# Level products of a chunked recurrence on four quadrants of TensorE, and rows of v turned once, stored and loaded by chunk

## The reference, cut to what matters

```python
def wkv_scan(s0, r, w, k, v, a, b, reverse):
    def step(s, inp):
        r_t, w_t, k_t, v_t, a_t, b_t = inp
        sa = jnp.einsum('bhvk,bhk->bhv', s, a_t)
        s = s * w_t[:, :, None, :] + sa[..., :, None] * b_t[:, :, None, :] \
            + v_t[..., :, None] * k_t[:, :, None, :]
        return s, jnp.einsum('bhvk,bhk->bhv', s, r_t)
```

## Time and profile before

| What | Value |
|---|---|
| median of 3 runs | 2602.45 us (2600.98 to 2603.02) |
| the profiled execution's own time | 2604.29 us |
| its span in the profile | 2602.5 us |
| its mean granted TensorE clock | 0.933 of full speed |
| PE busy over the span | 2314.5 us (89%) |
| DVE busy | 1688.6 us (65%) |
| ACT busy | 1025.3 us (39%) |
| POOL busy | 661.3 us (25%) |
| chunk loop, first to last `inverted` | 1407.4 to 1774.6 us |

### The profile page before, as it was taken

The page is one execution under the profiler, slowest core; times in us unless marked ns, Lnnn a source line. Parts: engine busy times, 40 slices in busy tenths (PEclk is TensorE's granted clock), DMA queues, the critical chain, the costliest instruction groups (busy, mean ns, idle before and its releaser), DMA issues. The chain is left out here.

```text
span 2602.5 us, 50127 instructions
## 1 busy us (share of the span) xinstructions
PE 2314.5 (89%) x20892; PEld 1847.3 (71%) x20892; DVE 1688.6 (65%) x2155; ACT 1025.3 (39%) x1633; POOL 661.3 (25%) x659
## 2 busy tenths in 40 slices
PE   5998988899999669999777999999973999999993
PEld 2886755568877558888636899997652888888883
DVE  5990559551115445666576776774657999999994
ACT  3112541231014420001154545444132877777773
POOL 1331568123320023222006666650000100000000
PEclk8998999999999779999878999998986999999997
DMA  6232004421104445211053111104142999999994
GB/s 237 96 124 75 1 33 142 132 99 45 49 14 185 151 156 193 96 41 40 14 185 92 32 32 29 29 20 169 57 174 97 409 407 396 396 393 405 396 378 158
DMA packets 136485, 401.77 MB, mean 154 GB/s; under 512 B 56314, under 2 KB 67834, under 8 KB 108754
## 3 DMA queue, kind: packets, MB, share of 16 engines
q1 hardware_dynamic: 124180, 360.02, 37.3%
q0 software_dynamic: 4608, 16.78, 2.7%
q10 hardware_dynamic: 7488, 21.99, 2.2%
HBM read 341.05 MB, written 57.69 MB: 153 GB/s over the span
## 5 line engine op out<-in xcount | busy, mean ns | idle before, releaser
L3900 DVE TENSOR_TENSOR ex_wl<-ew_raw,ex_wh 128x2048 fp32r<-128x2048 f32 x192 | 435.6, 2290 | 41.7 <-ACT ex_wh L3862 38.2
L3862 ACT ACTIVATE ex_wh<-ew_raw 128x2048 fp32r<-128x2048 f32 x192 | 367.6, 1919 | 109.5 <-PE ex_U L3806 40.3
L118 PE MATMUL sp_acc<-b2h_hi,sp_wh 128*128 128x512 f32 (+1 forms) x528 | 194.7, 369 | 16.2 <-POOL sp_wl L1729 16.2
L118 PE MATMUL sp_acc<-b2h_lo,sp_wh 128*128 128x512 f32 (+1 forms) x528 | 194.4, 368 | 0.0
L118 PE MATMUL sp_acc<-b2h_hi,sp_wl 128*128 128x512 f32 (+1 forms) x528 | 194.2, 368 | 0.0
L3783 POOL DMA_INDIRECT x<-ex_o,ex_at x16 | 26.5, 1656 | 490.2 <-DVE ex_o L3923 490.2
L2621 PE MATMUL rc_chain<-rc_x,rc_near 64*64 64x64 f32 x3200 | 132.8, 222 | 5.3 <-DVE rc_near L2503 2.2
L1727 POOL CAST sp_wh<-sp_w 128x1024 fp32r<-128x1024 f32 x26 | 28.3, 1088 | 402.2 <-DMA sp_w<-in_w_conv 221.4
L2621 PEld LDWEIGHTS rc_chain<-rc_x,rc_near 64*64 64x64 f32 x3200 | 111.1, 135 | 19.2 <-issue 9.0
L118 PEld LDWEIGHTS sp_acc<-b2h_hi,sp_wh 128*128 128x128 f32 x528 | 100.1, 190 | 33.9 <-POOL sp_wl L1729 16.6
L118 PEld LDWEIGHTS sp_acc<-b2h_lo,sp_wh 128*128 128x128 f32 x528 | 100.2, 190 | 16.4
(11 more groups left out here) (520 smaller groups left out, 5887.6 us busy)
## 6 DMA issues: line engine op xcount, KB each, us to landing
ew_raw<-in_exp_gate SPq DMA_DIRECT2D x64, 1024.0 KB, 8.0
ew_raw<-in_exp_up SPq DMA_DIRECT2D x64, 1024.0 KB, 9.5
ew_raw<-in_exp_down SPq DMA_DIRECT2D x64, 1024.0 KB, 8.0
b2p_pT<-in_ada_w SPq DMA_DIRECT2D x32, 512.0 KB, 6.0
rc_ac<-ac SPq DMA_DIRECT2D x40, 256.0 KB, 3.4
b_pj<-in_ada_w SPq DMA_DIRECT2D x8, 1024.0 KB, 12.5
ssm_wm<-in_w_merge SPq DMA_DIRECT2D x16, 512.0 KB
ac<-rp_ac SPq DMA_DIRECT2D x4, 2048.0 KB, 7.1
```

The costliest lines, as they stand in the source:

```text
L118: ins = nc.tensor.matmul(out, w[a][:, k, :], h[b][:, k, cols], start=(first and n == 0), stop=(last and n == 2))
L3862: nc.scalar.activation(wh[:, n % RING], raw[:, n % RING], ACT.Copy).then_inc(q["w_hi"], 1)
L3900: V.tensor_tensor(wl[:, n % RING], raw[:, n % RING], wh[:, n % RING].bitcast(f32), ALU.subtract).then_inc(q["w_lo"], 1)
```

## The change

In the levels, `diagonal` becomes `chain`. The eight products of a level stay, but the pairs of heads with j = 1 go through the two quadrants off the diagonal: `chained_x` takes them from rows p to partitions 1-p, and `advanced` takes them back. So for these heads `t1` and `xt` lie on swapped halves. A transpose on DVE is now three instructions: one of 128 partitions by 128 columns for the heads that stay, and two of 64 partitions by 128 columns for those that swap sides. PSUM is used in both banks of `X[d]` by each product.

The rows of v are turned in `rwkv_prepare`, ahead of the first `logits`: 40 transposes of 128x128 on TensorE, 10 copies of 128x512 on ACT, 10 stores of 256 KB to HBM (`v_rows`). In the chunk loop `v_staged`, `v_rows` on TensorE and the four `v_rows` copies on ACT are gone; SP issues 8 loads of 32 KB for a chunk (`load_v`), each once `state` of the chunk before and `outputs` have read `uv`.

The outputs from the state and from the chunk are summed in PSUM: `outputs` on TensorE takes both, in groups of four products of 64 rows and four of 128 rows, and `outputs_of_state` is gone on TensorE and on DVE. The orders of all engines are written anew.

```diff
+                for i in range(TILES):
+                    if i >= 6:
+                        pe.wait_ge(q["v_out"], i - 5)
+                    for b in range(HP):
+                        last = nc.tensor.transpose(acc[:, i % 6 // 2, i % 2, b * P:(b + 1) * P], pT[:, VB + b, i * P:(i + 1) * P], T.ident[:])
+                    last.then_inc(q["v_turned"], 1)
...
+                for i in range(TILES):
+                    act.wait_ge(q["v_turned"], i + 1)
+                    nc.scalar.activation(v_staged[:, i], acc[:, i % 6 // 2, i % 2], ACT.Copy).then_inc(q["v_out"], 1)
...
                     if u == 0:
+                        pe.wait_ge(q["v_out"], TILES)
...
+                def load_v(c):
+                    for d in range(2):
+                        if c:
+                            sp.wait_ge(joint["s_done"], c)
+                        if c > CTX_CK:
+                            sp.wait_ge(joint["y_crossed"], c - CTX_CK)
+                        for e in range(2):
+                            own = t[d]["uv"][e * CK:(e + 1) * CK].rearrange("p f (j a) t -> p f j a t", a=2)
+                            rows = v_dram[at(c, d):at(c, d) + CK, :].rearrange("r (j a f t) -> r f j a t", a=2, f=2, t=CK)
+                            for f in range(2):
+                                sp.dma_start(own[:, f, :, 1 - e, :], rows[:, f, :, 1 - e, :]).then_inc(q[d]["v_loaded"], 16)
...
-                        V.transpose(b["xt"][:].rearrange("p h t -> p (h t)"), b["x"][:, c % 2].rearrange("p h t -> p (h t)")).then_inc(s["xt_next"], 1)
...
+                        near_half, far_half = slice(0, 2), slice(2, 4)
+                        V.transpose(flat(b["xt"][:, near_half]), flat(b["x"][:, c % 2, near_half])).then_inc(s["xt_next"], 1)
+                        for p in range(2):
+                            src, to = slice(p * CK, (p + 1) * CK), slice((1 - p) * CK, (2 - p) * CK)
+                            V.transpose(flat(b["xt"][to, far_half]), flat(b["x"][src, c % 2, far_half])).then_inc(s["xt_next"], 1)
...
-                    for h, p in product(range(HP), range(2)):
-                        k = slice(p * CK, (p + 1) * CK)
-                        last = M(chained(d, bank)[k, h], l(h, p)[k], r[k, h], start=True, stop=True)
+                def quarters():
...
+                    for f, j, p in product(range(2), range(HP // 2), range(2)):
+                        yield 2 * j + f, j, f, p, p ^ j
...
+                def chain(d, back, l, r):
...
+                    for h, j, f, p, o in quarters():
+                        frm, to = (o, p) if back else (p, o)
+                        k = slice(frm * CK, (frm + 1) * CK)
+                        last = M(chained(d)[to * CK:(to + 1) * CK, j, f], l(h, p)[k], r[k, h], start=True, stop=True)
...
-                        each("v_rows", 2 * c + 2)
+                        each("v_loaded", 64 * (c + 1))
...
+                        for j, d in product(range(HP // 2), range(2)):
+                            b, at = t[d], slice((2 * d + j) * CK, (2 * d + j + 1) * CK)
+                            for e, f in product(range(2), range(2)):
+                                k, h = slice(f * CK, (f + 1) * CK), 2 * j + e
+                                M(W[k, e, at], b["S"][k, h], b["ar"][k, c % 2, h, CK:], start=True, stop=False)
+                            for e, f in product(range(2), range(2)):
+                                k, h = slice(f * CK, (f + 1) * CK), 2 * j + e
+                                last = M(W[k, e, at], b["uv"][:, f, h], b["near"][:, c % 2, f, 1, h], start=False, stop=True)
```

More of the change, by code:

```diff
@@ L2150, in rwkv_chunks @@
                 b[n] = ph.sb(f"{n}{d}", [P, HP, CK])
[L2151 removed]
+            for n in ("e_neg", "tmp", "t1", "g", "sum", "S"):
                 b[n] = ph.sb(f"{n}{d}", [P, HP, CK])
@@ L2438, in _ @@
+                    right_side(k - 2, 0)
                     right_side(k - 2, 1)
[L2439 to L2449 removed]
@@ new lines, in _ @@
+                    kept(k - 1, 1)
+                    kept(k - 1, 0)
+                    key_rows(k - 1, 0, 0)
+                    inverse(k - 2, 0)
+                    inverse(k - 2, 1)
+                    factored(k - 1, 0, 0)
+                    decay_in(k, 0)
+                    key_rows(k - 1, 1, 0)
+                    decay_in(k, 1)
+                    solved(k - 2, 1, 1)
+                    solved(k - 2, 1, 0)
+                    solved(k - 2, 0, 0)
+                    solved(k - 2, 0, 1)
@@ L2535, in right_side @@
                         V.tensor_tensor(b["g"][:], part(V_, d), b["g"][:], ALU.add).then_inc(s["g_ready"], 1)
-                def outputs_of_state(c, d):
-                    if runs(c, CTX_CK):
-                        n = c - CTX_CK
-                        dve.wait_ge(joint["y_done"], n + 1)
-                        for o in range(2):
-                            dve.wait_ge(q[o]["y_added"], 2 * n + 1)
-                        yv = y[:, :, y_at(c, d):y_at(c, d) + CK]
-                        V.tensor_tensor(yv, part(V_, d), yv, ALU.add).then_inc(q[d]["y_added"], 1)
                 def outputs(c, d):
@@ L2571, in _ @@
                     dve.sem_inc(q[d]["y_added"], 1)
-                for k in range(NCK + 1):
+                for k in range(NCK + 2):
+                    outputs(k - 2, 0)
+                    outputs(k - 2, 1)
+                    advanced(k - 1, 1, 0)
+                    advanced(k - 1, 0, 1)
+                    turned(k - 1, 1, 1)
+                    turned(k - 1, 0, 2)
+                    summed(k - 2, 0)
+                    summed(k - 2, 1)
+                    advanced(k - 1, 1, 1)
+                    advanced(k - 1, 0, 2)
+                    turned(k - 1, 1, 2)
+                    turned(k - 1, 0, 3)
+                    first(k, 1)
+                    advanced(k - 1, 1, 2)
+                    advanced(k - 1, 0, 3)
                     first(k, 0)
-                    advanced(k - 1, 0, 3)
-                    first(k, 1)
-                    advanced(k - 1, 1, 3)
+                    turned(k - 1, 1, 3)
                     last_factor(k - 1, 0)
                     turned(k - 1, 0, 4)
+                    advanced(k - 1, 1, 3)
                     turned(k - 1, 1, 4)
@@ L2749, in key_rows @@
                         last.then_inc(joint["rows_done"], 1)
-                def v_rows(c):
-                    if runs(c):
-                        each("v_staged", c + 1)
-                        if c < NCK - 1:
-                            each("rows_ready", 2 * c + 2)
-                        else:
-                            each("v_rows", 2 * c)
-                        for d in range(2):
-                            last = turned(part(Z, d), t[d]["vst"])
-                        last.then_inc(joint["v_done"], 1)
                 def state(c):
@@ L2775, in _ @@
                     chained_x(k - 1, 1, 0)
-                    advanced(k - 1, 0, 0)
-                    solved(k - 2)
+                    chained_x(k - 1, 0, 1)
+                    outputs(k - 2)
                     advanced(k - 1, 1, 0)
-                    chained_x(k - 1, 0, 1)
-                    outputs_of_state(k - 2)
+                    advanced(k - 1, 0, 1)
+                    state(k - 2)
                     chained_x(k - 1, 1, 1)
-                    advanced(k - 1, 0, 1)
-                    outputs(k - 2)
+                    chained_x(k - 1, 0, 2)
@@ L2794, in _ @@
-                    advanced(k - 1, 0, 3)
+                    chained_x(k - 1, 0, 4)
+                    right_side_of_state(k - 1)
                     advanced(k - 1, 1, 3)
+                    lower(k, 0)
+                    chained_x(k - 1, 1, 4)
+                    right_side(k - 1)
                     key_rows(k, 0)
-                    chained_x(k - 1, 0, 4)
-                    right_side(k - 1)
-                    chained_x(k - 1, 1, 4)
-                    lower(k, 0)
-                    right_side_of_state(k - 1)
+                    inverted(k - 1)
@@ L2804, in rwkv_output @@
+                    chained_x(k, 0, 0)
+                    lower(k, 1)
+                    solved(k - 1)
+                    advanced(k, 0, 0)
+                    key_rows(k, 1)
 def rwkv_output(nc, T, I, pT, y, bonus_dram, bonus, bx_dram, xmid, mod_dram, split, ow, ow_loaded, xm, row):
```

191 lines of the change are left out of this document (69 added, 122 removed).

## The result

| | median | lowest to highest | runs | ratio to before (95%) |
|---|---|---|---|---|
| before | 2601.72 us | 2599.82 to 2603.02 | 4 | 1 |
| changed | 2639.97 us | 2634.95 to 2644.66 | 4 | 1.0147 [1.0127, 1.0167] |

The changed kernel is slower by 38 us, where the prediction had it faster by 33; it is outside the range. The profiled execution took 2644.66 us with a span of 2642.9 us and a mean granted clock of 0.934, where it was 0.933 before.

The account below looks back on a forecast made before the run. TensorE was taken to bound the loop. Fifteen output intervals save 27 us, three context intervals and the first chunk 11, the tail 1.5, minus 7 for preparation: 33 less, 2569 us; range 2542 to 2598.

Parts of the forecast that it names:

- The transposes: On DVE, a 128-column transpose has a slot of 0.19 us, three 0.57; ten sets bring DVE to 15.7 a chunk.
- narrow transposes at the price of wide ones: Rival, chance 0.11: each narrow DVE transpose costs a wide one's slot, 2.4 us a chunk; kernel about 2616 us.
- slots follow columns: Argument about DVE steps: slot times go by column count; used for the 0.57 us and against the dear-transposes rival.
- The walk: One chunk followed from `inverted` through the engines' steps: 17.9 us with outputs, 15.2 without, small waits included.
- the tail 1.5: Term for the last loop interval, the one without a next chunk: 1.5 us saved.
- 0.5 for small waits: Added to each walked chunk: 0.5 us that TensorE's summed slots missed in the old output chunk.
- Level products on four quadrants: TensorE's level products take 0.26 us each on four quadrants, giving back 3.8 us of TensorE time a chunk.
- Outputs: TensorE's merged `outputs`: 2.0 us of products plus eight shape changes at 0.09, 2.75 us in all.
- Loads of v: SP's eight issues and a landing take 6.2 to 7.6 us against 7.3 available; cost taken as nothing.
- Preparation: `logits` waits for ten ACT copies of v, plus 7 us; bounds plus 5.6 and plus 9.
- that rival: Rival, chance 0.04: transposes of v lift the early preparation's clock from 0.50; kernel 2557 us.
- signs of being wrong: Three transposes over 0.8 us, ACT's list before `outputs` or SP's loads the last wait, or a clock falling in the loop.

Follow-up runs that it names:

- e2_two: Changed kernel with two 128x128 transposes in place of one 128x128 and two 64x128, far heads not swapped; 2622.3 us, ratio 1.0083.
- e12: e1_wide with uv double buffered and the loads of v waiting for a chunk earlier; 2605.9 us, ratio 1.0020.
- e13: Changed kernel, three transposes kept, with uv double buffered and the loads of v waiting for a chunk earlier; 2642.2 us, ratio 1.0160.
- e15: Changed kernel with level products on the two diagonal quadrants, one 128x256 transpose and uv double buffered; 2625.5 us, ratio 1.0093.
- e14: Kernel before with v turned in the preparation and loaded a chunk early into two uv; 2600.2 us, ratio 0.9999.
- e1_wide: Changed kernel with one 128x256 transpose in place of the three narrow ones, far heads not swapped; 2619.0 us, ratio 1.0070.
- e9_after_two_uv: Changed kernel with uv double buffered and the loads of v moved forward in SyncE's list; 2790.2 us, ratio 1.0723.

## Why the prediction failed

**The transposes: the first step that failed.** "A transpose of 128 columns then has a slot of 0.19, and three 0.57" rests on slots following columns, and the bounds of 0.45 to 0.96 for the three leave the measured 1.00 outside. In the rows that it came from every instruction starts at partition 0. The slot of 128 columns is right (0.21 in e2_two). What is wrong is that these three, in this succession, each wait for the end of the one before: 0.32 to 0.35 for each, 1.00 for a set and so 0.43 more than forecast, ten sets a chunk. Of the price, e12 and e13 give two points: 2606 at 0.33 a set and 2642 at 1.00. Read between them (an estimate, since the time need not be linear in it), a set of 0.57 would give 2619, so the mis-sized slot is worth about 23 us. The rival "narrow transposes at the price of wide ones" had the place and the sign, and I gave it 0.11; "slots follow columns", which I held against it, was the very thing under test. But its time, 2616, is not where the kernel came out, and its price was too high. It had six sets of a chunk without cover, which for the 0.67 us between e12 and e13 would be 4.0 us a chunk; measured were 36 us, 1.8 a chunk. At that price the transposes alone would have left 10 of the 33 us. It took the second step to make the kernel slower.

**The walk: the second step, and the dearer one.** By the same estimate the kernel would take 2619 with the transposes that I forecast, 50 us over 2569. In e12 the output chunk is 19.8 us in the mean of fifteen, where the walk has 17.9 even with slower transposes; the four intervals without outputs have a mean of 17.7 for 15.2. The last interval is 18.0 there and 22.0 in the changed kernel, where "the tail 1.5" makes 14.7 of it. The clock has little part in e12: it was 0.91 and 0.92 in two intervals and 1.00 in the others, at most 3.3 us (an estimate). From the rows of e12, against the walk: `outputs` starts 4.6 us behind `inverted` (forecast 4.1) and DVE has its result at 7.7 (7.1); the own-half products start at 14.6 (13.3), `right_side` at 17.7 (16.0), the next `inverted` at 19.3 (17.4). No single term is far off: 0.6 up to the result of `outputs`, 0.6 from there to the own-half products, 0.5 to `right_side`, 0.2 to the end. In the first of them `solved` stands behind `lower` on PE, from 1600.85 to 1601.94, where I had ScalarE set the pace and PE idle. So the step that failed is that the walk followed one engine at a time and then added 0.5 for small waits, taken from a loop in which PE was the bound. Where PE, DVE and ACT take turns, each wait shows. That the rewritten order costs time by itself is shown by e15 against e14, 25 us; which waits make up the rest I can't settle with these runs.

**Level products on four quadrants: right.** 0.24 for each, forecast 0.26, though they pair rows on one bank. TensorE's busy time fell. They are worth 20 us in this order (e15 against e12), not the 3.8 x 19 = 72 of TensorE time that they free: PE is busy for 98% of the loop in e15 and for 88% in e12, so it no longer bounds.

**Outputs:** 2.99 for 2.75, since by my 2.0 for the products a change of shape costs (2.99 - 2.0) / 8 = 0.12 and not 0.09 (an estimate): 3.6 us in fifteen chunks, a part of the walk's shortfall.

**Loads of v:** right in the changed kernel, for a reason that the forecast can't claim. Eight issues take 5.65 us there and up to 6.3 in other chunks, and land 2.3 later: 8.0 to 8.6, over my 6.2 to 7.6. The chunk had grown enough to hide it: `right_side` starts 9.4 us after the first issue, where the walk had 7.3. That is luck. In a chunk of the forecast length they would have been late; e1_wide, against e12, lost 13 us that way.

**Preparation:** forecast 7, measured 4.9 from `logits` to `logits`, 5.9 if the 1.0 us is added by which this execution reached the stage earlier (1279.19 against 1280.19 in the kernel before). From `logits` on the clock was 0.50, as said. While v was turned it was higher (0.90 between 1284 and 1290 us, where it was 0.50 before), so the transposes did lift it, as that rival had it, but it was back at 0.50 when `logits` started, and nothing was gained.

**The sum:** 2569, less 1 for the preparation, plus about 51 for the walk and about 23 for the transposes, is 2642, which is e13 and, with v hidden, the changed kernel. The sum closes by construction, since the walk's part is what the others leave over. Of the prediction's signs of being wrong, the transposes came (1.00 against 0.8), and the clock fell in the loop, though only in the last interval.

## What to carry to other kernels

When a DVE step is split so that its parts start at different partitions, price each part at its whole duration and not at its columns, and look at what precedes and follows it. When a change takes work off the bounding engine, walk the new chunk over all engines' lists at once, and don't carry over the small waits of the old loop, where the bound hid them. Read the granted clock by stretches: it fell where an engine kept PE waiting, and a mean over the kernel didn't show it. A load that waits for a buffer belongs behind everything in its queue that is wanted earlier, or in another queue; a second buffer helps only if the wait in the queue is weakened too.

## What was unexpected about the hardware

- A 128-column transpose on DVE started 0.21 to 0.24 us behind one that starts at the same partition, and 0.29 to 0.35 behind one that doesn't.
- The issue of a 32 KB load of v took 0.60 us in the median and 5.3 to 6.3 for eight in a row. That is more for each than the 0.52 of a 256 KB load of `ac`.
- PE goes from level products to `outputs` and eight times between its two shapes without a wait, and each change costs about 0.12 us (an estimate, as above).
- The granted clock fell from 1.00 to 0.50 within the loop while PE idled for 7.73 us in e9_after_two_uv, and in the last interval of the changed kernel after pauses of at most 1.35 us.
